# A decoder step with routed experts: picks in number order, overflow ahead of the last experts, the final sum in pairs, and four smaller edits

## The reference

```
mixed = (sigmoid(ga) * (o_mla @ w_mla_o) + sigmoid(gb) * (ret @ w_ret_o)) @ w_out
h     = layer_norm(ALPHA * x + mixed, ln1_g, ln1_b)
eidx, ew = route(h, w_router, router_bias)         # 6 of 64 experts and their weights
ffn   = sum_k ew[k] * swiglu(h, expert eidx[k]) + swiglu(h, shared)
y     = layer_norm(ALPHA * h + ffn, ln2_g, ln2_b)
```

## Time and profile before

| | us |
|---|---|
| median of 3 runs | 1817.27 |
| lowest, highest | 1810.52, 1817.49 |
| the profiled execution | 1811.45 |
| its span | 1809.3 |
| TensorE busy | 1737.8 (96%) |
| VectorE busy | 1072.8 (59%) |
| ScalarE busy | 677.6 (37%) |
| GpSimd busy | 332.6 (18%) |

### The profile page before, as it was taken

The page is one execution under the profiler, slowest core; times in us unless marked ns, Lnnn a source line. Parts: engine busy times, 40 slices in busy tenths (PEclk is TensorE's granted clock), DMA queues, the critical chain, the costliest instruction groups (busy, mean ns, idle before and its releaser), DMA issues. The chain is left out here.

```text
span 1809.3 us, 27137 instructions
## 1 busy us (share of the span) xinstructions
PE 1737.8 (96%) x9448; PEld 1332.4 (74%) x9448; DVE 1072.8 (59%) x1730; ACT 677.6 (37%) x1092; POOL 332.6 (18%) x282
## 2 busy tenths in 40 slices
PE   7999999999999999999997889999999999999996
PEld 7999999999955555998874466767676767676633
DVE  3112442635346565745686557777777777777568
ACT  3112222312154554212110145656565656565411
POOL 0000321403010000000146432222222222222112
PEclk9999999999999999999999899999999999999998
DMA  6333543444123123625260589999999999999697
GB/s 206 94 92 93 154 117 124 129 126 144 62 78 95 37 70 133 236 78 171 84 246 3 185 298 367 396 384 400 410 399 390 395 393 381 390 398 361 224 378 313
DMA packets 140352, 408.65 MB, mean 226 GB/s; under 512 B 29316, under 2 KB 90916, under 8 KB 120676
## 3 DMA queue, kind: packets, MB, share of 16 engines
q1 hardware_dynamic: 116052, 338.02, 50.9%
q0 software_dynamic: 21344, 52.59, 7.6%
q10 hardware_dynamic: 2880, 17.04, 2.3%
HBM read 359.78 MB, written 67.80 MB: 236 GB/s over the span
## 5 line engine op out<-in xcount | busy, mean ns | idle before, releaser
L2651 PE MATMUL e_Y<-mixT,e_aT 128*128 128x512 f32 x544 | 246.9, 597 | 6.4 <-issue 5.3
L2662 PE MATMUL e_G<-w_lo,xT_hi 128*128 128x512 f32 x528 | 205.8, 390 | 0.0
L2651 PEld LDWEIGHTS e_Y<-mixT,e_aT 128*128 128x128 f32 x544 | 103.4, 191 | 112.2 <-issue 107.2
L2509 DVE TENSOR_TENSOR w_lo<-wb,e_w_hi 128x1024 fp32r<-128x1024 f32 x132 | 155.0, 1220 | 19.4 <-ACT e_w_hi L2429 19.4
L2509 DVE TENSOR_TENSOR w_lo<-wb,half_hi 128x1024 fp32r<-128x1024 f32 x128 | 150.5, 1221 | 12.5 <-ACT half_hi L2429 12.2
L2502 DVE TENSOR_TENSOR xT_lo<-e_T,xT_hi 128x1024 fp32r<-128x1024 f32 x66 | 80.8, 1225 | 127.7 <-ACT xT_hi L2424 127.6
L1299 PE MATMUL banks<-x_hi,gw_hi 128*128 128x352 f32 x464 | 151.5, 327 | 1.4 <-DVE r_srg L1091 1.4
L183 PE MATMUL banks<-w_hi,x_hi 128*128 128x244 f32 x512 | 143.3, 280 | 9.7 <-DVE x_lo L237 8.9
L1299 PE MATMUL banks<-x_lo,gw_hi 128*128 128x352 f32 x464 | 148.8, 321 | 0.0
L1299 PE MATMUL banks<-x_hi,gw_lo 128*128 128x352 f32 x464 | 148.8, 321 | 0.0
L2424 ACT CAST xT_hi<-e_T 128x1024 fp32r<-128x1024 f32 x66 | 67.1, 1017 | 202.7 <-PE e_T L2640 202.7
(11 more groups left out here) (433 smaller groups left out, 3604.9 us busy)
## 6 DMA issues: line engine op xcount, KB each, us to landing
wb<-in_w_exp_gu SPq DMA_DIRECT2D x64, 2048.0 KB
mixT<-in_w_exp_dn SPq DMA_DIRECT2D x68, 1024.0 KB
yk<-d_y_rows SPq DMA_DIRECT2D x16, 1536.0 KB, 18.8
gw_sb<-in_w_gate SPq DMA_DIRECT2D x20, 512.0 KB, 6.6
d_proj<-o_sb SPq DMA_DIRECT2D x8, 1098.0 KB, 5.7
d_gateT<-r_g_out ACTq DMA_DIRECT2D x16, 528.0 KB, 2.6
pages<-in_cache_both SPq DMA_DIRECT2D x64, 128.0 KB, 2.0
wb<-in_w_exp_gu ACTq DMA_DIRECT2D x4, 2048.0 KB
```

What stands on the lines that cost most here:

```text
L2509: v.tensor_tensor(w_lo[s][:, :, at_k, :], w_gu[s][:, :, at_k, :], w_hi[c][:, :, at_k, :].bitcast(F32), ALU.subtract).then_inc(w_lo_ok, 1)
L2651: mm = t_.matmul(Y[q][:], aT[:, c, k, :], w_d[:, s, k, q * 512:(q + 1) * 512], start=k == 0, stop=k == 1)
L2662: mm = t_.matmul(G[c], x[:, c, k, :], w[:, :, k, :], start=k == 0 and i == 0, stop=k == KD - 1 and i == 2)
```

## The change

1. **project.** Twelve matmuls on cleared data run ahead of the first real one. VectorE and ScalarE take tiles 0 and 1 out of PSUM between the fifth and the sixth tile of `x`, instead of behind the ninth.
2. **attention.** For the last two half chunks one sum of 128 partitions (`turned_whole`) and four DMAs from SP take the place of four sums; `sample_queries` moves from item 1 to item 3.
3. **router.** `choose` puts the six picks in the falling order of their experts' numbers (one copy and three `max` more for each of three groups). `place(1)` and `build(1)` go ahead of `swished(0)` and `gated(0)`.
4. **order of items.** Experts 0 to 59, then the overflow, then experts 60 to 63. A token's picks 4 and 5 then lie among the items ahead of the last four, whatever the data, and picks 2 and 3 among those up to expert 61. All 52 overflow lists are loaded in the first four rounds of the loop, three or four behind each refill.
5. **the end.** The rows are read in pairs into 14 places as soon as they are written and as a place is free: pair 2 and a part of pair 1 during the last four experts. TensorE adds two rows of a tile, VectorE four. `diag` is made by GpSimd, ahead of its last two scatters. The norm's `scaled` of the first seven tiles goes to ScalarE (scale) and GpSimd (bias).

```diff
@@ project
+            pe.wait_ge(cleared, 1)
+            for _ in range(WARM):       # WARM = 12
+                nc.tensor.matmul(banks[:, 7, 0:CW], o_sb[:, 0, NT - 1, 0:P], o_sb[:, 0, NT - 1, :], start=True, stop=True)
...
-            for t in range(1, NT):
+            for t in range(1, 5):
                 residue(t)
+            evac_one(dve, v.tensor_copy, 0, free_by_dve, dve_out, 0)
+            for t in range(5, NT):
+                residue(t)
@@ attention
+            for x in (4, 5):
+                sp.wait_ge(r_sum, x - 3)
+                for j in range(4):
+                    sp.dma_start(qT[64:96, 4 * (x % 2) + j, 2 * TC:3 * TC], rt[32 * j:32 * j + 32, x % 2, 0]).then_inc(r_moved, 16)
             load_pages(0)
...
+            def turned_whole(x):
+                dve.wait_ge(r_mul, 2 * x + 2)
+                v.tensor_tensor(rt[:, x % 2, 0], rt[:, x % 2, 0], rt[:, x % 2, 1], ALU.add).then_inc(r_sum, 1)
@@ trunk, choose and the order behind it
+                link(v.tensor_copy(f8[:, :, 0:TOPK], i8[:, :, 0:TOPK]))
+                for t in range(G):
+                    ins = v.max(by_number[:, t, :], f8[:, t, :])
+                link(ins)
...
             choose(1)
+            place(1)
+            build(1)
             swished(0)
             gated(0)
-            place(1)
-            build(1)
             choose(2)
@@ experts, sync
-            with sp.Fori(2, OVER // W + 2) as r:
+            PER = OVER // W
+            with sp.Fori(2, 2 + W) as r:
                 for s in range(W):
                     refill(r, s, sp.snap(r * W + s))
-                    overflow_list(sp.snap(r * W + (s - 2 * W)))
+                    for b in range(PER * s // W, PER * (s + 1) // W):
+                        overflow_list(sp.snap(r * PER + (b - 2 * PER)))
+            with sp.Fori(2 + W, NE // W - 1) as r:
+                for s in range(W):
+                    refill(r, s, sp.snap(r * W + s))
...
+            weights_read(0)
+            rows_written(NE - W)
+            pair(0, 2)
+            pair(1, 2)
...
+            rows_written(NE - W + 2)
+            pair(0, 1)
+            weights_read(3)
+            for t in range(1, 5):
+                pair(t, 1)
+            small_pair(1)
+            h_tiles(2)
+            h_tiles(3)
+            h_tile(NT - 1)
+            for t, passed_on in ((5, 0), (6, 1), (7, 2)):
+                sp.wait_ge(added, added_at(passed_on, 2))
+                pair(t, 1)
+            rows_written(NE)
+            small_pair(0)
...
@@ experts, gpsimd
+                if s == W:
+                    wait_alone(pool, xT_dve, pool.snap(more * W + (NE - 2)))
+                    wait_alone(pool, gu_done, pool.snap(more * W + NE))
+                    for lo in (0, 4):
+                        k = 2 * pair_on_pe(lo)
+                        g.tensor_tensor(diag[:, lo:lo + 4], ident..., w_tok[:, lo:lo + 4, k:k + 2]..., ALU.mult).then_inc(diag_ok, 1)
                 put_rows(at(pool, r, W, s - 1), s % 2, (s - 2) % W)
...
+                if i < BY_POOL:             # BY_POOL = 7
+                    pool.wait_ge(spread_ok, i + 1)
+                    g.tensor_tensor(acc[0:n, t, :], acc[0:n, t, :], b2[0:n], ALU.add).then_inc(biased, 1)
@@ experts, scalar
+            def spread(i):
+                act.wait_ge(gained, i + 1)
+                act.wait_ge(rstd_ok, i + 1)
+                s_.activation(acc[0:n, t, :], acc[0:n, t, :], ACT.Copy, scale=rstd[0:n, t:t + 1]).then_inc(spread_ok, 1)
@@ experts, vector, the end
+            for t in range(5):
+                add(t, 1)
+            join(0)
+            mean(0)
+            for i in range(1, NT):
+                if i <= 3:
+                    add(i + 4, 1)
+                elif i <= 7:
+                    add(i, 0)
+                variance(i - 1)
+                gain(i - 1)
                 join(i)
                 mean(i)
-                if i:
+                if i > BY_POOL:
                     scaled(i - 1)
@@ experts, tensor
-                for k in range(ON_PE):      # ON_PE = 3
+                for k in range(2):
```

More of the change, by code:

```diff
@@ L292, in _, with body @@
             s_.copy(w_hi[:, 0, H:], w_sb[:, 0, H:]).then_inc(w_rounded, 1)
-            for t in range(1, NT):
+            for t in range(1, 5):
                 rounded(t)
-            def body(r, last=False):
+            evac_one(act, s_.copy, 1, free_by_act, act_out, 0)
+            for t in range(5, NT):
+                rounded(t)
+            def body(r, last=False, first=0):
                 def between(j):
@@ new lines, in small_pair, with rows_written, weights_read @@
+            def small_pair(j):
+                for k in (2 * j, 2 * j + 1):
+                    sp.dma_start(pairs[SMALL][NS * (k % 4):NS * (k % 4 + 1), k // 4, :],
+                                 y_rows.rearrange("(t k) n -> t k n", k=8)[(NT - 1) * P:(NT - 1) * P + NS, k, :]).then_inc(pair_in[SMALL], 16)
+            def rows_written(n):
+                for c in range(2):
+                    wait_alone(sp, y_out[c], sp.snap(more * (8 * W) + 8 * n))
+            def weights_read(s):
+                wait_alone(sp, gu_done, sp.snap(more * W + (NE - W + s + 1)))
@@ new lines, in _ @@
+            weights_read(1)
+            pair(3, 2)
+            pair(4, 2)
+            h_tiles(0)
+            wait_alone(sp, x_turned, sp.snap(more * (2 * W) + 2 * NE))
+            pair(5, 2)
+            weights_read(2)
+            pair(6, 2)
+            pair(7, 2)
+            small_pair(2)
+            h_tiles(1)
+            rows_written(NE - W + 2)
+            pair(0, 1)
+            weights_read(3)
+            for t in range(1, 5):
+                pair(t, 1)
+            small_pair(1)
@@ new lines, in _ @@
+            h_tiles(2)
[6 more added lines that the diff above has]
+            small_pair(0)
+            sp.wait_ge(added, added_at(3, 2))
+            pair(0, 0)
+            for t in range(1, 6):
+                sp.wait_ge(added, added_at(t - 1, 1))
+                pair(t, 0)
+            for t in (6, 7):
+                sp.wait_ge(pe_done, t - 5)
+                pair(t, 0)
@@ new lines, in add_row @@
+            def add_row(t, k):
+                u, use = place_of[t, k // 2]
+                assert ADD_ORDER[n_added[0] // 2] == (t, k // 2) and n_added[0] % 2 == k % 2
+                if t not in tile_added:
+                    dve.wait_ge(acc_in[t], 16)
+                else:
+                    dve.wait_ge(added, tile_added[t])
+                dve.wait_ge(pair_in[u], 16 * use)
+                v.scalar_tensor_tensor(acc[:, t, :], pairs[u][:, k % 2, :], w_part[:, t, k:k + 1], acc[:, t, :], ALU.mult, ALU.add).then_inc(added, 1)
+                n_added[0] += 1
+                tile_added[t] = n_added[0]
@@ new lines, in add, with small_weights @@
+            def add(t, j):
+                add_row(t, 2 * j)
+                add_row(t, 2 * j + 1)
+            def small_weights():
+                dve.wait_ge(part_ok, 1)
+                for k in range(TOPK):
+                    own = slice(NS * (k % 4), NS * (k % 4 + 1))
+                    dve.wait_ge(small_w_ok, k + 1)
+                    v.tensor_scalar(diag_small[own, k // 4, :], ident[own, own], w_small[own, k // 4:k // 4 + 1], None, ALU.mult).then_inc(small_ok, 1)
+            with dve.Fori(1, NE // W - 2) as r:
@@ L2551, in _ @@
+            dve.wait_ge(lists_ok, 5)
+            v.tensor_scalar(list_g[:, NE - W:], list_s[:, NE - W:], 3, None, ALU.logical_shift_right).then_inc(lists_ok, 1)
+            dve.wait_ge(lists_ok, 6)
+            with dve.Fori(NE // W - 2, more + (NE // W - 1)) as r:
                 four(r)
+            v.tensor_scalar(w_part[:], w_tok[:], 1.0 / ALPHA, None, ALU.mult).then_inc(part_ok, 1)
+            for k in range(TOPK):
+                own = slice(NS * (k % 4), NS * (k % 4 + 1))
+                v.tensor_copy(w_small[own, k // 4:k // 4 + 1], w_tok[0:NS, NT - 1, k:k + 1]).then_inc(small_w_ok, 1)
@@ L2559, in _ @@
             kept(at(dve, r, W, 0), 1)
[L2561 to L2568 removed]
+            add_row(3, 5)
             def join(i):
```

204 lines of the change are left out of this document (98 added, 106 removed).

## The result

| | before | after |
|---|---|---|
| median, us | 1816.17 | 1915.89 |
| lowest, highest | 1810.52, 1817.49 | 1913.27, 1917.44 |
| profiled execution, span | 1811.45, 1809.3 | 1913.27, 1911.5 |

What follows compares the result with a forecast made beforehand. TensorE and DMA were taken to bound the experts together, with SP's queue becoming the bound for 16 items; 43 - 12 - 2.1 - 2.5 - 0.5 = +26 us gave 1840 us, range 1795 to 1882.

Steps and rivals of the forecast that it cites:

- Lists: Experts' stage: lists packed in SP's queue make 16 items take 13.55 us each instead of 10.04, 43 us late.
- The cover: Experts' stage: weights issued well ahead of use absorb 13 us of SP's lateness, once for all 16 items.
- The upper end of 84: Experts' stage: with every list at 4.65 us, the 16 items end 84 us late after cover.
- rival C: Experts' lists keep their full price of before: 84 - 17 = +67 us, 1882 us; chance 0.15.
- The end: After the experts: small rows land at 1736, TensorE bounds at 6.86 us a tile, 12 us less.
- it stays under 6.86: End: GpSimd's work per tile, with a bias add of 1.2 to 3.7 us, stays under TensorE's 6.86 us.
- If the idle TensorE drops to half clock: End: a bound in which this, or small rows landing late, leaves only 7 us less.
- Start: Project: warm-up matmuls and early evacuation give 2.1 us less, bounds 1 more and 3 less.
- Attention: Attention: eight ops of 32 partitions become two of 128, 0.5 us less, bounds 1.5 less and 0.5 more.
- Router: Router: place(1) and build(1) partly fill VectorE's 10.5 us wait, 2.5 us less, bounds 1.8 more and 10 less.

Runs made afterwards that it cites:

- bias_add_narrow: lists_spread with GpSimd's bias add cut from 1024 to 128 columns, ScalarE's scaling kept: 1810.05 us, 1.0078 of the kernel before.
- spread_norm_on_vector: lists_spread with the norm's end on VectorE for every tile, no ScalarE scaling or GpSimd bias add: 1824.52 us, 1.0068 of the kernel before.
- adds_behind_gate: spread_norm_on_vector with VectorE's four pair adds moved behind the last item's gate product and the last output copies: 1.0064 of the kernel before.
- start_and_rope: The kernel before with only the start's (project) and the rope's (attention) parts of the change, without the router's: 0.9994.
- start_alone: The kernel before with only the start's part: twelve matmuls ahead of the first real one and the first two evacuations earlier: 0.9984.
- lists_spread: The changed kernel with the 52 overflow list loads standing one behind each refill again: 1829.89 us, 1.0093 of the kernel before.
- front_alone: The kernel before with only the front of the change (start, rope, router), lists and end as before: 1809.31 us, 0.9969; repeated, 0.9985.
- lists_packed_alone: The kernel before with only its 52 list loads packed 13 per round into rounds 2 to 5: 1910.75 us, 1.0538.
- rows_in_order_of_use: adds_behind_gate with the scattered rows queued, and VectorE's adds of them done, in the order of use: 1801.82 us, 1.0027 of the kernel before.
- lists_packed_one_load: lists_packed_alone with the four rounds written out without a loop, one register load per list instead of two: 1799.06 us, 1.0026 of the kernel before.

## Why the prediction was wrong, step by step

- **Lists: the mechanism right, a term mis-sized.** SP's queue does bound 16 items, ScalarE does wait for `wb`, and the period is 10.04 again behind them. From the first of the 16 weight issues (1071.84) to the next behind them (1338.0) it is 266.2 us, 16.6 us an item where I had 13.55, and 49 us in all. By term: the first list of an item I had at 4.6 and it is 8.05; the second at 4.2 and it is 3.13; the others at 3.0 and they are 2.7: together 232.6 us for the 52 where I had 200.8, 32 more. The work apart from lists was 1.5 us and not 1, 8 more, and once, in the first item, SP waited 9.1 us for `d_done`. That is the 49. The price of the first list fell outside both of my bounds, since I had bounded it by rows of before, and there SP was never late. My reason for the 4.6 even named the 3 MB ahead of it, but then took the price from rows with 1 MB just issued and the other 2 MB 4.9 us old in the median. The kernel before held the warning: its own lists grow from 4.1 to 5.3 us as that age falls from over 5.5 to 3.
- **The cover** was right: 105.6 us later at the issues, about 93 later in the experts (95.4 less the 2.1 that the second item happened to differ), so 12 us were absorbed, 13 forecast.
- **The upper end of 84**, rival C, was the nearest. The mean list costs 4.47 us after and 4.53 before: one dear list and two cheap ones come to the old price. What it lacked of the 93 are the 0.5 us an item and the wait of 9.1, less what a list was cheaper.
- **The end: wrong in sign.** TensorE's 6.87 us a tile and VectorE's two adds at 2.6 are right where nothing disturbs them (bias_add_narrow). Three steps failed. (a) The queue ahead of the small rows: I counted from 1709 on and had 11 MB at 410 GB/s. In fact, in spread_norm_on_vector, whose rows go the same way, the DMA engines were full from 1700 on, 19.45 MB passed from there to 1755 at 354 GB/s, and SP could issue the small rows only 14.9 us behind the last down projection, when the last scatter (at 5.9) had been written through the same full engines; before, the two stand at 6.5 and 2.2. The small rows landed at +35.7 in after, where I had +20.3: 15.4 us. (b) "it stays under 6.86": I priced GpSimd's bias add by its own duration (3.01, bounds 1.2 to 3.7) and never by what it does to VectorE; by bias_add_narrow that is 5.5 us (one trace each, on two chips). (c) Three adds ahead of the last `gated` I left out altogether. They took 7.0 us and not 3.8, since GpSimd made `diag` beside two of them (2.80 and 2.92 us each for 1.28), and made the last item 7.5 us longer. By adds_behind_gate the small rows come no earlier without them, so (a) and (c) are one delay: counted from the start of the last item the small rows began at 66.8 us where I had 43.9.
- **"If the idle TensorE drops to half clock"** came true: the granted clock was 0.50 in the wait, the lower of the two levels, and the small tile's eight matmuls took 6.07 us instead of the 3.71 of the earlier trace rows, which is 2.4 us. With (a) and (b) that is 23.3, and the end missed my forecast by 22.9 (+10.9 for -12).
- **Start: right.** 2.1 us in the trace and 0.9984 in time (2.9 us, interval 0.5 to 5.4); start_and_rope, which has the same edit, is at 0.9994 with 1 inside its interval.
- **Attention: no gain seen.** +0.5 in the two traces, its upper bound, where I had given -0.5; start_and_rope is no faster than start_alone. A half microsecond can't be read from these runs.
- **Router: the size is the chip's.** -10.1 us in the traces was my lower bound, but most of that isn't the edit's: on one chip the stage took 215.5, 210.7 and 215.5 us with the edit (lists_spread, spread_norm_on_vector, front_alone) and 215.1 without it (lists_packed_alone). I had taken the 10.5 us of the earlier trace rows for a property of the kernel; on four of the five chips of the experiments it isn't there. The whole front is worth 5.6 us on that chip (5.1 forecast) and 2.7 on another.
- **The chances.** 0.63 for slower was right; 0.15 for C (+67) was too little, and nothing was left for more. The result lies 34 us above the upper end of the range: the lists cost 9 us more than C's 84, and the end, which stood in C as -12 too, came as +18 with the last item's 7.5.

## What to carry to other kernels

A queue that is hidden has two prices for what stands in it, one while it runs ahead and one once it is late; ask for the second before packing work into it, since being late can itself raise it. An address that the queue can know at build time saves a load: here it cut the price of the same packing from 96 to 5 us. A transfer that is wanted first must be queued by what stands ahead of it in bytes, not by when it is issued, and rows fetched early are paid for by whatever lands behind them. Work moved to an idle engine is priced by what the neighbour does meanwhile too. And a wait read on one chip can be that chip's own.

## What the runs showed of the hardware

- A register load behind 3 MB of just issued weights takes 4.5 us and the dependent one 2.5 (means of 16); for the third list of an item, when the DMA engines are nearly idle (share 0.10), it is 1.06 and 0.62.
- DMA engines busy for a full share moved 240 to 430 GB/s. The size of the packets doesn't explain it: in rows_in_order_of_use those of 4 KB took 159 ns from 1704.5 to 1709 (426 GB/s in all) and 276 ns from 1714 to 1720 (246 GB/s), and those of 8 KB, alone from 1728.5 to 1736, 314 ns (421 GB/s). The 12 KB packets of the end of before took 464 ns (428 GB/s, 1745 to 1755), and 846 where the small rows were in flight (1730.5 to 1732). Transfers of the small tile's rows land in or right behind the slow stretches (1714.5, 1717.7, 1725.2 and 1728.3 in rows_in_order_of_use); what slows the rest there isn't shown. So fetching two rows of a token at a time instead of three has almost no price of its own, 421 against 428 GB/s.
- VectorE's two adds take 4.58 us beside a bias add of 3.01 us on GpSimd and 2.60 without it.
- The same stage of the same code takes 202 us on one chip and 215 on another, and one instruction of ScalarE begins 0.04 or 9.7 us behind the matmul that it waits for (lists_packed_one_load, lists_packed_alone).
